# A two-layer hybrid trunk step: the output projection goes tile by tile, and the second norm, transposes and router logits move in between its later parts

## The reference, cut to what matters

```python
def mixer(h, lp, ...):
    ...                                   # attention, SSD scan, conv module
    out = jnp.concatenate([attn, y, u], axis=-1) @ lp['w_out']      # (640, 1024) @ (1024, 1024)
    return out, ...

def rms_norm(x, w):
    y = x * lax.rsqrt(jnp.mean(x * x, axis=-1, keepdims=True) + EPS)
    return y * w

def trunk_layer(x, cond, lp, ...):
    sh1, sc1, g1, sh2, sc2, g2 = modulation(cond, lp['mod_w'], lp['mod_b'])
    mix, ... = mixer(rms_norm(x, lp['norm1']) * (1 + sc1) + sh1, lp, ...)
    x = x + g1 * mix
    x = x + g2 * hierarchical_moe(rms_norm(x, lp['norm2']) * (1 + sc2) + sh2, lp)

def hierarchical_moe(x, lp):
    g_logits = xt @ lp['rg_w'] + lp['rg_b']         # 4 group logits a token
    e_logits = xt @ lp['re_w'] + lp['re_b']         # 32 expert logits a token
    ...                                   # top-1 group, top-2 experts, gated MLPs of 32 experts
```

## Time and profile before

| | |
|---|---|
| Time, median of 3 runs | 1556.58 us (1556.3 to 1564.58) |
| Time of the profiled execution | 1551.64 us |
| Its span in the profile | 1549.9 us |
| PE busy | 1270.1 us (82%) |
| DVE busy | 710.0 us (46%) |
| ACT busy | 278.0 us (18%) |
| Mean DMA rate | 216 GB/s |
| Mean granted clock of PE | 0.914 of full speed |

### The profile page before, as it was taken

One profiled execution on the slowest core, in us unless ns is written; L12 is line 12 of the kernel. 1 busy time (PEld: TensorE's weight loads), 2 busy tenths in 40 slices (PEclk: granted clock), 3 DMA queues, 4 the chain that ended last, 5 costly groups with the idle time before them and its releaser, 6 DMA issues.

```text
span 1549.9 us, 20431 instructions
## 1 busy us (share of the span) xinstructions
PE 1270.1 (82%) x7740; PEld 874.6 (56%) x7740; DVE 710.0 (46%) x1518; ACT 278.0 (18%) x698; POOL 109.6 (7%) x162
## 2 busy tenths in 40 slices
PE   4699999879878589968829999988897567998692
PEld 1565577548764256635427556765687444675350
DVE  3156866781255123322352686678325512332124
ACT  1120233650111000000022004266211000000000
POOL 1000000001000111111000000000100011111000
PEclk9899999999958899988969999999996679999896
DMA  9221101342237999999750210024511099999985
GB/s 389 88 76 54 65 1 55 143 192 97 84 143 307 414 420 421 418 414 408 311 225 33 81 55 27 22 96 158 211 55 69 37 419 420 420 419 413 401 348 229
DMA packets 57958, 334.63 MB, mean 216 GB/s; under 512 B 11184, under 2 KB 11184, under 8 KB 23668
## 3 DMA queue, kind: packets, MB, share of 16 engines
q1 hardware_dynamic: 42340, 294.96, 47.1%
q0 software_dynamic: 15520, 38.36, 6.5%
HBM read 322.42 MB, written 27.62 MB: 226 GB/s over the span
## 4 chain that ended last, share of the span: by engine, by line
PE 51%; DMA 24%; DVE 9%; SPq 4%; issue 4%; ACT 2%; DVEq 2%; PEld 1%; PEldq 1%; ACTq 0%; POOL 0%; POOLq 0%
DMA U<-in_stream 12%; PE bank L1563 11%; PE bank L1827 9%; DMA ring<-in_stream 8%; PE bank L1508 8%; PE bank L1919 6%; PE bank L1953 5%; SPq L344 4%; PE bank L1841 2%; DMA U<-moe_out 1%; PE bank L1664 1%; PE bank L1810 1%; DMA CAT<-moe_in,gidx 1%; DVE U L1145 1%; PE bank L1604 1%
## 5 line engine op out<-in xcount | busy, mean ns | idle before, releaser
L1919 PE MATMUL bank<-U,HT 128*64 128x256 f32 (+2 forms) x1056 | 185.5, 413 | 32.9 <-DMA U<-in_stream 16.6
L1563 PE MATMUL bank<-HT,ring 128*128 128x512 f32 (+1 forms) x640 | 175.4, 435 | 2.0 <-issue 2.0
L1508 PE MATMUL bank<-ring,HT 128*128 128x256 f32 x640 | 151.2, 389 | 12.7 <-ACT HT L592 12.6
L1919 PEld LDWEIGHTS bank<-U,HT 128*64 128x64 f32 (+2 forms) x1056 | 116.6, 150 | 78.9 <-issue 53.3
L1919 PE MATMUL bank<-ring,HT 128*64 128x256 f32 (+2 forms) x832 | 140.7, 416 | 22.9 <-DMA U<-in_stream 18.5
L1827 PE MATMUL bank<-ring,HT 128*128 128x256 f32 x640 | 142.5, 386 | 8.2 <-issue 8.2
L1563 PEld LDWEIGHTS bank<-HT,ring 128*128 128x128 f32 x640 | 97.3, 191 | 79.7 <-issue 79.7
L1827 PEld LDWEIGHTS bank<-ring,HT 128*128 128x128 f32 x640 | 123.7, 194 | 26.7 <-issue 9.4
L1508 PEld LDWEIGHTS bank<-ring,HT 128*128 128x128 f32 x640 | 120.8, 194 | 29.1 <-issue 13.6
L1919 PEld LDWEIGHTS bank<-ring,HT 128*64 128x64 f32 (+2 forms) x832 | 94.2, 157 | 51.8 <-issue 33.9
L985 DVE SCALAR_TENSOR_TENSOR U<-U,prm 128x655 f32<-128x655 f32 x120 | 107.8, 898 | 7.0 <-issue 1.3
(11 more groups left out here) (341 smaller groups left out, 1660.1 us busy)
## 6 DMA issues: line engine op xcount, KB each, us to landing
ring<-in_stream SPq DMA_DIRECT2D x158, 1024.0 KB, 21.5
U<-in_stream SPq DMA_DIRECT2D x96, 1024.0 KB, 30.4
RAB<-in_stream SPq DMA_DIRECT2D x12, 1024.0 KB, 30.3
U<-moe_out SPq DMA_DIRECT2D x20, 512.0 KB, 7.3
RAB<-mod_rows POOLq DMA_DIRECT2D x12, 512.0 KB, 7.7
moe_in<-CAT POOLq DMA_DIRECT2D x10, 512.0 KB, 2.9
X<-in_x SPq DMA_DIRECT2D x1, 2560.0 KB
out_y<-X SPq DMA_DIRECT2D x5, 512.0 KB, 6.9
```

What stands on the lines that cost most here:

```text
L1508: ins = e.matmul(bank[:, 256 * h:256 * h + 256], HT[:, k, t * P:(t + 1) * P], wt(q)[:, k, :], start=(k == 0), stop=(k == KD - 1))
L1563: ins = e.matmul(out, wt(q)[:, k, P * (n % 2):P * (n % 2) + P], HT[:, k, lo:lo + w], start=(k == 0), stop=(k == KD - 1))
L1919: ins = e.matmul(PS[2 + p][s, FF * j:FF * j + FF], xgT[:, p, k, s], wt(key)[:, k, :], start=(k == 0), stop=(k == KD - 1))
```

## The change

- **Projection**: piece n is now half n % 2 of tile n // 2, so a token tile is complete after every second piece. Both halves' ring slots are freed at the last tile, after pieces 8 and 9.
- **Matrix engine's order**: pieces 0 to 5, transposes of tiles 0 and 1, piece 6, logits of tiles 0 and 1, pieces 7 to 9, transposes of tiles 2 and 3, logits 2, transposes 4, logits 3 and 4. The logits go to bank 7.
- **Norm**: in three groups, tiles 0 and 1, tiles 2 and 3, tile 4. `sq_rdy` is raised after the squares of pieces 3, 7 and 9. VectorE runs `rs` three times on two, two and one columns instead of once on five, and writes both passes of a row to `CAT`, with no buffer `mt`. These stand between the residual additions.
- **RC**: its two instructions and the wait `ld_rows` now stand after piece 1, not piece 5.
- **Copies into HT**: ScalarE copies both banks of a transposed tile (`h2_out`); VectorE's `evac2` is gone.

```diff
-                    t, hf = n % NT, n // NT
                     e.wait_ge(S["x_added"], 10 * l + n + 1)
-                    A(sqtmp, X[:, t, 512 * hf:512 * hf + 512], ACT.Square, accum_out=small(1600 + n, 1))
+                    A(sqtmp, X[:, n // 2, 512 * (n % 2):512 * (n % 2) + 512], ACT.Square, accum_out=small(1600 + n, 1))
                     e.drain()
-                e.drain().then_inc(S["sq_rdy"], 1)
+                    if n in (3, 7, 9):
+                        e.drain().then_inc(S["sq_rdy"], 1)
+                    if n == 5:
+                        h2_out(0)
+                        h2_out(1)
+                for t in range(2, NT):
+                    h2_out(t)
...
+                residual(0)
+                residual(1)
+                e.wait_ge(S["ld_rows"], 80 * (l + 1))
+                for cc in range(2):
+                    e.scalar_tensor_tensor(out=RC[:, cc, :], in0=RC[:, cc, :], scalar=1.0, in1=nrow2, op0=ALU.add, op1=ALU.mult)
+                for t in (0, 2):
+                    residual(2 * t + 2)
+                    residual(2 * t + 3)
+                    y = norm2(t, 2, 1 + t // 2)
+                    h2_row(t, y[:, 0:1])
+                    residual(2 * t + 4)
+                    h2_row(t + 1, y[:, 1:2])
+                    residual(2 * t + 5)
+                h2_row(4, norm2(4, 1, 3))
...
+                def h2_row(t, y):
+                    e.scalar_tensor_tensor(out=CAT[:, t, :], in0=X[:, t, :], scalar=y, in1=RC[:, cnd(t), :], op0=ALU.mult, op1=ALU.mult); dr()
+                    e.tensor_tensor(CAT[:, t, :], CAT[:, t, :], RB[:, cnd(t), :], ALU.add).then_inc(S["h2_rdy"], 1)
...
+                for n in range(6):
+                    projected(n)
+                h2_turned(0)
+                h2_turned(1)
+                projected(6)
+                logits(0)
+                logits(1)
+                for n in range(7, 10):
+                    projected(n)
+                h2_turned(2)
+                h2_turned(3)
+                logits(2)
+                h2_turned(4)
+                logits(3)
+                logits(4)
```

More of the change, by code:

```diff
@@ L269, in build @@
                  "cum_sb dec_rdy gt_ps gt_sb r_ps l_rdy w_rdy xd_rdy y_ps y_sb off_ps off_sb hs_rdy st_rdy "
-                 "ut_ps ut_sb ct_ps ct_sb_a ct_sb_d wo_ps wo_sb st_ps gated h2_rdy h2_st h2T_ps h2T_a h2T_d lg_ps lg_sb "
+                 "ut_ps ut_sb ct_ps ct_sb_a ct_sb_d wo_ps wo_sb st_ps gated h2_rdy h2_st h2T_ps h2T_a lg_ps lg_sb "
                  "soft_x soft_y m_rdy rank_ps slot_rdy slot_ps gidx_rdy "
@@ L1185, in _, with residual @@
                 e.wait_ge(S["ld_g1"], 32 * (l + 1))
-                for n in range(2 * NT):
-                    t, hf = n % NT, n // NT
+                halves = small(1600, NT, 2)
+                def residual(n):
+                    t, k = n // 2, slice(512 * (n % 2), 512 * (n % 2) + 512)
                     e.wait_ge(S["wo_ps"], 10 * l + n + 1)
-                    e.tensor_tensor(wtmp[:, n % 2, :], PS[4 + n % 2][:], RA[:, cnd(t), 512 * hf:512 * hf + 512], ALU.mult
-                                    ).then_inc(S["wo_sb"], 1)
-                    dr()
-                    e.tensor_tensor(X[:, t, 512 * hf:512 * hf + 512], X[:, t, 512 * hf:512 * hf + 512], wtmp[:, n % 2, :], ALU.add
-                                    ).then_inc(S["x_added"], 1)
-                    if n == 5:
-                        e.wait_ge(S["ld_rows"], 80 * (l + 1))
-                        for cc in range(2):
-                            e.scalar_tensor_tensor(out=RC[:, cc, :], in0=RC[:, cc, :], scalar=1.0, in1=nrow2, op0=ALU.add, op1=ALU.mult)
@@ L1215, in _, with norm2 @@
-                evac2(NT - 1)
+                    e.tensor_tensor(wtmp[:, n % 2, :], PS[4 + n % 2][:], RA[:, cnd(t), k], ALU.mult).then_inc(S["wo_sb"], 1)
+                    dr()
+                    e.tensor_tensor(X[:, t, k], X[:, t, k], wtmp[:, n % 2, :], ALU.add).then_inc(S["x_added"], 1)
+                def norm2(t0, n, signal):
+                    e.wait_ge(S["sq_rdy"], 4 * l + signal)
+                    e.tensor_tensor(small(1400, n), halves[:, t0:t0 + n, 0], halves[:, t0:t0 + n, 1], ALU.add); dr()
+                    return rs(n, 1.0 / D)
@@ L1802, in _, with turned_tile @@
                 e.wait_ge(S["fill_sb"], mod_chunks(l, 0) + 2)
-                def turned_tile(t, signal, a, d_, order):
+                def turned_tile(t, signal, taken, order):
                     if t >= 2:
-                        e.wait_ge(S[a], NT * l + t - 1)
-                        e.wait_ge(S[d_], NT * l + t - 1)
+                        for name in taken:
+                            e.wait_ge(S[name], NT * l + t - 1)
                     for i, k in enumerate(order):
@@ L1817, in _, with projected @@
                 e.wait_ge(S["fill_sb"], mod_chunks(l, 0) + MODC // 2)
-                for n in range(2 * NT):
-                    t, hf = n % NT, n // NT
-                    q = b + INN + MODC + 2 * hf
+                rw = pr("rw", KD, 36)
+                def projected(n):
+                    t, q = n // 2, b + INN + MODC + 2 * (n % 2)
                     arrived(q)
@@ L1832, in _, with h2_turned @@
                             e.drain().then_inc(free[slot_of(q + j)], 1)
-                rw = pr("rw", KD, 36)
-                e.wait_ge(S["wo_sb"], 10 * (l + 1))
+                def h2_turned(t):
+                    e.wait_ge(S["h2_rdy"], NT * l + t + 1)
+                    turned_tile(t, "h2T_ps", ("h2T_a",), range(KD))
                 def logits(t):
                     e.wait_ge(S["h2T_a"], NT * l + t + 1)
-                    e.wait_ge(S["h2T_d"], NT * l + t + 1)
                     for k in range(KD):
-                        ins = e.matmul(PS[4][:, 36 * t:36 * t + 36], HT[:, k, t * P:(t + 1) * P], rw[:, k, :], start=(k == 0), stop=(k == KD - 1))
+                        ins = e.matmul(PS[7][:, 36 * t:36 * t + 36], HT[:, k, t * P:(t + 1) * P], rw[:, k, :], start=(k == 0), stop=(k == KD - 1))
                     if t == NT - 1:
                         ins.then_inc(S["lg_ps"], 1)
-                for t in range(NT):
-                    e.wait_ge(S["h2_rdy"], NT * l + t + 1)
-                    turned_tile(t, "h2T_ps", "h2T_a", "h2T_d", range(KD))
-                    if t:
-                        logits(t - 1)
-                logits(NT - 1)
+                for n in range(6):
[13 more added lines that the diff above has]
+                logits(4)
                 MM = small(900, NT, NE)
                 mods, q1 = MODBANK[1], b + INN + MODC + OUTN
+                e.wait_ge(S["wo_sb"], 10 * (l + 1))
                 chunk(mods[0], q1)
```

28 lines of the change are left out of this document (8 added, 20 removed).

## The result

| | device time, median (range, runs) |
|---|---|
| before | 1558.22 us (1556.3 to 1564.58, 4) |
| changed | 1541.38 us (1538.96 to 1545.48, 4) |
| changed, measured again | 1537.26 us (1532.18 to 1542.43, 6), beside before at 1557.98 |

Sign and range held; the value of 1532.9 was 4 to 8.5 us too low. The profiled execution of the changed kernel took 1545.48 us, with a span of 1543.7.

The account below looks back on a forecast made before the run. It took the chain of waits as the bound, with a 34.32 us tail behind the tenth piece in each layer. 17.46 - 5.61 = 11.85 us, twice 23.7, against 1556.58 gave 1532.9 us, range 1520 to 1545.

Parts of the forecast that it names:

- pieces 7 to 9 at 6.9 us each with the granted clock at 1.00: Projection behind the inserted logits: expected sign in the changed profile that the full clock holds, 6.9 us a piece.
- the clock falls at the inserted work: Rival: thin matmuls between projections lower PE's clock; gain 7 to 10 us a layer, 1537 to 1543 us, chance 0.19.
- the 11.85 us: Each layer's forecast gain: 17.46 us leaving the tail less 5.61 us inserted before piece 9.
- tail that is left: From the tenth handover to the routing: 8.20 us to transposes 4 plus a last round of 8.66, together 16.86 us.
- transposes and logits inserted: Tiles 0 and 1 before piece 9: transposes 1.74 us and 32 logit passes 3.87 us, 5.61 us later.
- the tail keeps the full clock: Rival: PE stays at 2.4 GHz, last round 4.7 us instead of 8.66; 1525 us, chance 0.08.
- A logit pass at full clock 0.121: Inserted logits: 0.121 us a pass, taken from the 37-column form, with 0.109 as the bound from below.
- VectorE has 2.1 us to spare: Before the tenth residual: VectorE finishes row 3 at 425.4, piece 9 comes at 427.5, so VectorE is not late.
- The earlier RC and the later slots cost nothing: RC after piece 1 has 3 us of cover; weight slots freed after piece 8 have 30 us of cover.
- Each shortening reaches the end: Behind the stage: an earlier `lg_ps` moves everything forward; the rival, given back behind, 1550 to 1557 us, had 0.07.
- The clock falls and does not come back: Slower rival: pieces 7 to 9 at 1.2 GHz, 13.8 us each instead of 6.9; 1580 us, chance 0.04.
- 17.46 taken out and 5.61 put in: Per layer: 17.46 us of work leaves the 34.32 us tail, 5.61 us goes between projections before piece 9.

Follow-up runs that it names:

- experiment 4: Changed kernel with logits of tile 1 moved from behind piece 6 to behind piece 7, apart from those of tile 0; 1535.29 us, ratio 0.9847.
- 9: The kernel of experiment 4 with the first modulation chunk, 32 wide passes, pulled in front of transposes 4; 1526.54 us, ratio 0.9815.
- 10: Changed kernel with logits 0 and 1 moved behind transposes 2 and 3, half of the first modulation chunk behind each; 1526.52 us, ratio 0.9791.
- kernel 3: Kernel before with only the order of pieces changed, tiles instead of halves on all three engines; 1559.53 us, ratio 1.0005.
- kernel 11: Kernel before with nine wide matmuls, results unused, put behind piece 9 in PE's wait for the norm; 1540.02 us, ratio 0.9888.
- 12: kernel 6 with half of the first modulation chunk put behind the transposes of tile 1, in PE's pause; 1520.69 us, ratio 0.9763.
- 5: Changed kernel with logits of tiles 0 and 1 moved behind piece 9 and transposes 2 and 3; 1528.3 us, ratio 0.9805.
- kernel 6: Changed kernel with all transposes and logits behind piece 9, alternating, norms and rows still early; 1522.27 us, ratio 0.9793.
- kernel 7: kernel 6 run again, nothing edited; 1532.98 us, ratio 0.9811.
- kernel 8: kernel 6 with logits 0 and 1 side by side and transposes 2 and 3 side by side; 1524.86 us, ratio 0.9799.

## Why the prediction was right, and where it was off

The step that failed is, in the prediction's words, "pieces 7 to 9 at 6.9 us each with the granted clock at 1.00". The clock fell to a mean of 0.60 behind the two logit tiles, and pieces 7 and 8 took 15.5 us instead of 13.8. The forecast gave 0.62 to a clock that stays, and 0.19 to the rival "the clock falls at the inserted work", 1537 to 1543 us, which is what happened, at its lower price and in both layers. The stated range of 1520 to 1545 held because it had been drawn to take in that rival; of the forecast's own 1527 to 1538 the first median, 1541.38, lies outside. The sum of layer 0, term by term:

| term | forecast | measured | adds to the 11.85 us |
|---|---|---|---|
| tail that is left | 16.86 | 16.71 | +0.15 |
| transposes and logits inserted | 5.61 | 1.75 + 3.49 = 5.24 | +0.37 |
| pieces 7 and 8 behind them | 13.8 | 15.5 | -1.7 |
| pieces 0 to 5 | as before | 1.0 longer | -1.0 |
| stage | 94.12 | 96.33 | 9.64 left (9.67 by the terms) |

The 1.7 is from the traces of the changed kernel and of experiment 4: from transposes 0 to the tenth handover 35.44 us (398.62 to 434.06) and 33.77 (393.78 to 427.55). The 1.0 stands in three of the changed kernel's four stages and in one of the four of before, and over all 14 traces in 11 of 28 stages, in either order of the pieces, so it is likely chance and not the change. With a stage of 93.68 in layer 0 (95.05 in layer 1, with the 1.0 in it), experiment 4 is nearest to the kernel that the forecast described, 94.12, and it took 1535.3 us against 1532.9.

- *Tail of 16.9, at 0.50.* Right: 16.71 and 17.05. In layer 1 the pause before transposes 4 was 2.89 us instead of 2.54. The last round was 8.67 us, as in the earlier trace rows. Up to the last pause the tail ran at 0.98, and only the last round at 0.50; kernels 9 and 10 show that filling that wait brings it to 1.00, for the 4 us of the round that the rival "the tail keeps the full clock" had worked out.
- *A logit pass at full clock 0.121.* It is 0.109 (3.49 / 32), the lower bound.
- *VectorE has 2.1 us to spare.* It was 2.51, and PE's pause came from L1213 and not from the copies.
- *The earlier RC and the later slots cost nothing.* Right; kernel 3, which has the later slots and not the earlier RC, is at 1.0005, and the changed kernel's RC instructions start at 372.58 with no idle time before them.
- *Each shortening reaches the end.* Right in the main: stages shorter by 18.6 us (kernel 11), 37.1 (12), 30.0 (5) and 23.2 (4) went with medians lower by 18.6, 34.8, 29.7 and 22.7. The largest shortfalls are those of kernels 6 and 10, 38.5 and 34.4 us of stage with 33.7 and 29.4 of time. For 6 the tail differs between executions, as kernel 7 showed; for 10 the cause stays open.
- *The clock falls and does not come back.* Not in the projection, in any trace. It does in a tail (kernel 7), a place that I had not asked about.
- *What the gain is from.* The prediction, like the change, counted work taken out of the tail and put between projections. Kernels 4 to 6 show that this part loses: PE sets the pace in both places, and each inserted microsecond comes back as one, with the clock on top. The forecast's two terms, 17.46 taken out and 5.61 put in, were each right in size, but the second bought nothing. What gained was that VectorE's norms and rows lay under the projection, and that PE's wait of 8.2 us went away or was filled, which spares the clock.

What stays open: why the clock falls behind 1.36 us of pause in one tail of four and not in the others; what share of kernel 6's tail is due to ScalarE's taking over the copies; and why the clock's dips in unchanged code, with which the rest of the span varies by up to 12.7 us, come in one execution and not in another.

## What to carry to other kernels

Ask of work that is moved under another engine's work whether its own engine is idle there; between two matmuls PE is not, and the move gains only through what is released earlier. Read the granted clock beside every stretch of PE, and price a wait of PE by the speed of what follows it too: unused wide work in the old kernel's wait was worth as much as the whole change, and a chunk that is due anyway, put into the new kernel's wait, took 2.8 us a layer off the tail. And compare stages between fixed marks before comparing spans, since two single executions of one kernel can differ by more than the edit.

## What was not expected of the hardware

- PE busy without a gap loses the clock: at the end of 3.5 us of passes of 36 columns it fell (15.3 to 15.75 us for the next 64 passes instead of 13.8), in 4 of 4 stages of the changed kernel, and between the pieces it did not fall behind 1.75 us of them, in 4 of 4 stages of kernels 4 and 9.
- The same alternation of transposes and logits runs at 1.00 for 15.16 us or at 0.50 for 24.82, by the level at which it begins; the earlier trace rows show only the slow one, and the forecast priced the last round by it.
- Sixteen transposes, at half speed for 3.50 us with nothing else on PE, were followed by 1.00 (kernel 8, both layers).
